# Two transformer blocks in one kernel: the second block's convolution columns go ahead of its token-shift projection

## The reference

```python
h = rms_norm(x, g[0])
p = h @ w_in_first                                   # 1024 -> 1024 + 1792 columns
y_conv = conformer_conv(p[..., :1024], ...)          # gate, 31-tap causal convolution per channel, layer norm, silu
y_rwkv, _ = rwkv7_mix(p[..., 1024:], mu, ...)        # token shift, then a recurrence over 8 heads of 64
y = concat([y_conv, y_rwkv]) @ w_out
x = x + rms_norm(y, g[1])
x = x + rms_norm(memory_cross_attention(...), g[3])
x = x + rms_norm(swiglu(...), g[5])
```

## Time and profile before

| | us |
|---|---|
| median of 3 runs | 1769.77 |
| lowest, highest | 1768.31, 1774.12 |
| the profiled execution | 1775.78 |
| span of its profile | 1773.7 |
| PE busy in the span | 1669.8 (94%) |
| DVE, ACT, POOL busy | 835.0, 605.4, 401.6 |

### The profile page before, as it was taken

One profiled execution on the slowest core, in us unless ns is written; L12 is line 12 of the kernel. 1 busy time (PEld: TensorE's weight loads), 2 busy tenths in 40 slices (PEclk: granted clock), 3 DMA queues, 4 the chain that ended last, 5 costly groups with the idle time before them and its releaser, 6 DMA issues.

```text
span 1773.7 us, 26856 instructions
## 1 busy us (share of the span) xinstructions
PE 1669.8 (94%) x11510; PEld 1373.4 (77%) x11510; DVE 835.0 (47%) x1240; ACT 605.4 (34%) x973; POOL 401.6 (23%) x349
## 2 busy tenths in 40 slices
PE   7999999999999999999898777998989899999997
PEld 6789878787888888888676666877868878888876
DVE  3377642445333333345666886635543442233234
ACT  4143432324323232343434442333434332222222
POOL 2112111112201010132135531004203431131133
PEclk7899999999999999999999889898999999999999
DMA  5123321223222222222211000014102122222221
GB/s 193 61 83 127 136 72 67 76 92 131 86 100 91 97 93 95 95 95 106 97 53 68 25 2 2 9 42 164 51 24 84 60 95 98 92 96 95 96 77 66
DMA packets 29830, 146.03 MB, mean 82 GB/s; under 512 B 4097, under 2 KB 7441, under 8 KB 14609
## 3 DMA queue, kind: packets, MB, share of 16 engines
q1 hardware_dynamic: 29712, 144.33, 23.3%
HBM read 138.03 MB, written 6.29 MB: 81 GB/s over the span
## 4 chain that ended last, share of the span: by engine, by line
PE 75%; DVE 8%; issue 7%; POOL 5%; ACT 4%; DMA 1%; POOLq 0%; SPq 0%; DVEq 0%; ACTq 0%
PE ps L153 75%; POOL zf L165 4%; DVE zf L165 2%; DVE zf L173 2%; DVE wl L165 1%; ACT zf L159 1%; ACT zr L162 1%; DVE ps L173 1%; ACT zf L162 1%; DMA raw<-in_wstream 1%; POOL tn L165 1%; ACT wh L162 1%; PE ps L156 0%; DVE zf L2326 0%; DVE zr L173 0%
## 5 line engine op out<-in xcount | busy, mean ns | idle before, releaser
L153 PE MATMUL ps<-zr,wh 128*128 128x512 f32 (+1 forms) x3936 | 1175.2, 383 | 24.7 <-DVE wl L165 13.2
L153 PEld LDWEIGHTS ps<-zr,wh 128*128 128x128 f32 x3936 | 717.8, 190 | 184.2 <-issue 11.9
L153 PE MATMUL ps<-zr,wl 128*128 128x512 f32 (+1 forms) x1968 | 745.7, 379 | 0.0
L165 POOL TENSOR_TENSOR zf<-zf 128x512 f32<-128x512 f32 (+1 forms) x253 | 295.8, 1176 | 862.0 <-ACT zf L159 581.1
L153 PEld LDWEIGHTS ps<-zr,wl 128*128 128x128 f32 x1968 | 374.1, 190 | 77.2 <-issue 0.8
L165 DVE TENSOR_TENSOR wl<-raw,wh 128x1024 fp32r<-128x1024 f32 (+1 forms) x243 | 306.4, 1300 | 231.2 <-ACT wh L162 231.0
L162 ACT ACTIVATE wh<-raw 128x1024 fp32r<-128x1024 f32 (+1 forms) x243 | 240.4, 1037 | 212.0 <-PE ps L153 210.4
L159 ACT ACTIVATE zf<-zf 128x512 f32<-128x512 f32 (+2 forms) x232 | 127.5, 560 | 399.1 <-DVE zf L165 285.1
L153 PE MATMUL ps<-zf 64*64 64x64 f32 (+6 forms) x3640 | 204.5, 249 | 34.3 <-DVE zf L165 18.7
L153 PEld LDWEIGHTS ps<-zf 64*64 64x64 f32 (+3 forms) x3640 | 163.2, 151 | 75.2 <-issue 29.1
L165 DVE TENSOR_TENSOR zf<-ps,zf 128x512 f32<-128x512 f32 (+2 forms) x133 | 84.1, 638 | 208.9 <-PE ps L153 185.6
(11 more groups left out here) (94 smaller groups left out, 725.9 us busy)
## 6 DMA issues: line engine op xcount, KB each, us to landing
raw<-in_wstream SPq DMA_DIRECT2D x117, 1024.0 KB, 4.8
zf<-in_xT SPq DMA_DIRECT2D x16, 256.0 KB, 3.1
raw<-in_wstream SPq DMA_DIRECT2D x4, 768.0 KB, 4.3
kv_scratch<-zf SPq DMA_DIRECT2D x8, 256.0 KB, 2.2
x_scratch<-zf SPq DMA_DIRECT2D x8, 256.0 KB, 2.1
zf<-x_scratch SPq DMA_DIRECT2D x8, 256.0 KB, 5.1
out<-zf SPq DMA_DIRECT2D x16, 128.0 KB, 1.7
zf<-in_cu SPq DMA_DIRECT2D x1, 1256.0 KB, 10.0
```

Of the source, the lines that this page charges most:

```text
L153: return self.raw.matmul(out_, l, x, start=start, stop=stop)
L165: return self.raw.tensor_tensor(out_, a, b, o)
```

## The change

```diff
-PFIRST = 3
...
+    for c in range(4):
+        t("cv", "w_in_first_2", 0, 8, (128 * c, 512 + 128 * c))
     for i in range(7):
         t("p", "w_in_first_2", 0, 8, [1024 + 128 * P_ORDER[2 * i + j] for j in range(2)])
-        if i == PFIRST - 1:
-            for c in range(4):
-                t("cv", "w_in_first_2", 0, 8, (128 * c, 512 + 128 * c))
...
-    for i in range(4):
-        put("ev.p", i)
-        pl.rel("D", "t.p", i)
-        if i:
-            p_tile(i - 1)
+    for i in range(2):
+        for j in range(2):
+            put("ev.cv", 2 * i + j)
+            pl.rel("D", "t.cv", 2 * i + j)
+        put("cv.mix", i)
+        mark("hc", i)
...
-            for tap in range(LAST[i] + 1):
-                while tap == LAST[i] and i > 1 and not has(("pdone",)):
-                    yield
+            for tap in range(LAST[i] if i > 1 else LAST[i] + 1):
                 put("tap.v", i, tap)
                 yield
+            if i == 1:
+                pl.rel("M", "conv.acc", i)
+        while not has(("pdone",)):
+            yield
+        for i in range(2, 4):
+            put("tap.v", i, LAST[i])
             pl.rel("M", "conv.acc", i)
+            yield
...
-    pl.pace[cv1], pl.pace[cv2] = 4, 3
+    pl.pace[cv1], pl.pace[cv2] = 6, 4
...
-    due = 3
-    for uu in range(2, 7):
-        if uu == PFIRST:
-            for i in range(4):
...
-            pl.pace[cv1] = 3
+    for i in range(2, 4):
+        n = pl.next_unit("cv")
+        pl.tile(n, 0, 2 * i)
+        if i == 3:
+            put("cv.mix", 2)
+            mark("hc", 2)
+        pl.tile(n, 1, 2 * i + 1)
+    pl.pace[cv1] = 4
+    due = None
+    for uu in range(7):
```

More of the change, by code:

```diff
@@ L515, in p_tile @@
         mark("p", P_ORDER[i])
-    n = pl.next_unit("p")
+    n = pl.next_unit("cv")
     pl.pair(n, 0)
@@ L523, in schedule @@
     put("pset")
-    n = pl.next_unit("p")
-    pl.take("D", "t.p", 2)
+    n = pl.next_unit("cv")
+    pl.take("D", "t.cv", 2)
     put("mm", n, 0, 2, 0)
@@ L528, in schedule @@
     put("mm", n, 0, 2, 1)
-    pl.take("D", "t.p", 3)
+    pl.take("D", "t.cv", 3)
     put("mm", n, 1, 3, 0)
@@ L756, in schedule @@
                 p_tile(due)
-            if i == 2 * PFIRST:
+            if i == 0:
                 put("cv.mix", 3)
```

## The result

| | before | after |
|---|---|---|
| median, us | 1771.0 (4 runs) | 1802.6 (4 runs) |
| lowest, highest | 1768.3, 1774.1 | 1801.2, 1804.6 |
| profiled execution, its span | 1775.8, 1773.7 | 1803.4, 1801.4 |

The account below looks back on a forecast made before the run. PE was taken as the bound, busy 94% of the span, with 75.5 us lost in a 389 us stretch. Waits of 26 and 51 us made 77, so +1.5 on the median of 1769.8: 1771 us, range 1751 to 1788.

Parts of the forecast that it names:

- the rule: A DVE operation with two SBUF inputs and a GpSimd operation exclude each other; one waits out the other's whole instruction.
- rival 3: POOL's additions block DVE's weight splits beside the dense tiles: 15 us, giving 1786 us; chance 0.08.
- A: First part of the second block's recurrence before the change, 819 to 991 us, holding 20 dense tiles.
- The waits of A': The first part after the change, keeping its 20 dense tiles: 146 us of work plus 26 of waits, 172 us.
- Weight splits, 5 us: Beside the dense tiles, weight remainders come 1 to 2.5 us late for three or four units: 5 us.
- The norm of pair 0, 12.5 us: At `prep`'s norm for pair 0, PE waits for ACT, ACT for DVE's scan behind its queue: 12.5 us.
- Transposes and banks, 5 us: `head 0` turns on three M banks instead of four, so products wait for evacuations: 5 us.
- Clock, 3.5 us: Work lost to PE's lowered clock beside the dense tiles, half of the earlier 6 us lost: 3.5 us.
- B' 20, C' 3, T' 28: Waits in 12 rounds without dense work, then 18 with it, then the last 19 without: 20, 3 and 28 us.
- Rival 2: The naked end, from the second quarter of `wb` on, loses 42 us instead of 28: 1785 us; chance 0.23.
- Rival 1: DVE's lag never reaches PE, so the part with the dense tiles takes 156 us: 1755 us; chance 0.33.
- The sum of +1.5 us: Over the whole stretch, waits total 77 us instead of 75.5, so the change costs 1.5 us.

Follow-up runs that it names:

- e5: Changed kernel with each of POOL's convolution additions replaced by eight zero fillings of 128x128: 1780.8 us, ratio 1.0033.
- e1: Changed kernel with POOL's convolution additions on 64 of 512 columns, the rest left out: 1777.0 us, ratio 1.0025.
- e18: Changed kernel with additions on 64 columns and two instead of four DVE taps per tile beside the projection: 1771.3 us, ratio 0.9990.
- e2: Kernel before the change with POOL's convolution additions on 64 of 512 columns, the rest left out: 1764.3 us, ratio 0.9953.
- e3: Changed kernel with each of POOL's convolution additions replaced by two zero fillings of 128x512: 1779.9 us, ratio 1.0045.

## Why the prediction was wrong

- *The step that failed* is the weighing of the rule, and with it rival 3: "Nine splits in A times 1.64 us (4.00 less 2.36) are 15 us: 1786. One in nine did so now, which speaks against." The one in nine was taken for a chance. It was the phase between ACT's queue and POOL's additions in the old order, and the change replaces this order. The trace of before had it, in rows of ACT and POOL that I did not read beside the earlier trace rows: POOL's row of 2.72 us from 901.62 ends 0.15 us after the remainder starts at 904.19. Nor could every remainder have met one: in A's trace there are ten pairs, and the first four start before POOL's first addition, at 877.04.
- *Its size.* Contention costs the changed kernel 27.3 us (ratios 1.0179 and 1.0025 of 1771), the kernel before 8.3 (0.9953), so the move pays 19 of its 32 us for it (17 by the medians). Of its sign, remainders of 4 us in most units, came four of ten above 4 us and two more at 3.4 and 3.5. Rival 3 counted remainders only, at 15; they took 34.7 us in A' where 24.4 is free (e5), 10 more. It left out the `x2` products (5.1 us, which now meet additions), the token shifts, the gates, the scan and products of `prep`, and POOL's own delay.
- *The waits of A'* were 62.2 us for 26: 13.4 at the splits, 17.3 at the norm of pair 0, 15.4 of other idling and 16.1 by the clock, for 5, 12.5, 5 and 3.5. PE's work was 142.4 for 146. The four items below take them in turn, with e1 beside them.
- *Weight splits, 5 us:* 13.4 in the waits, with 3.5 in e1, where hardly anything blocks. The sum of DVE's load was near.
- *The norm of pair 0, 12.5 us:* 17.3, and 10.2 in e1. Near for the kernel that was summed; e18 shows that 6.9 of the 10.2 hang on DVE's taps.
- *Transposes and banks, 5 us:* all other idling in A' is 15.4 us, and 11.7 in e1, so this was short in either case. Two waits behind the norm, for ACT and for DVE, are 4.4 and 4.2 of it. What of them is the third bank was not tested.
- *Clock, 3.5 us:* 16.1, and 10.0 in e1. This term was short in either case. PE's clock stood at half for 54.6 us of A', after the long waits, where it was 13.6 before.
- *B' 20, C' 3, T' 28:* 20.3, 2.0 and 21.8. Rival 2, whose point was 60 us from the second quarter of `wb` on, got 52.4 and falls. Rival 1 falls with the norm's wait.
- *The sum of +1.5 us* describes a change that meets no contention, made against a kernel that has it. e1, with A' 177.2 for 172, comes out at +4.4 us. There is luck in that: its waits in A' are 35.4 us and not 26, its work is 4 us less than forecast, and T' waits 21.7 and not 28.

What is left of the move without additions is 12.7 us (e1 against e2). The taps beside the projection are about half of that, as e18 takes 5.7 away. The other half was not taken apart.

## What to carry to other kernels

Where DVE and POOL share work, list DVE's operations with two inputs in SBUF and see, in the order of the engine that feeds POOL, what POOL does when each is issued: a reordering can turn meetings that are rare (one pair in ten here) into common ones (six in ten). Count the lock on both sides, since what is taken from DVE's wait comes back as POOL's and through whoever waits for POOL. And try the move with the suspected work made short in both kernels; here two such runs (e1, e2) put a number on a rival that had been given 0.08.

## What the hardware showed that I had not expected

- In a split two engines alternated instruction by instruction: each DVE piece waited out one addition (2.29 and 2.31 us for 1.22) and each addition one piece (1.84 and 2.09 for 1.27).
- The blocked time stands inside the instruction's own duration, and no idle time and no releaser is shown for it. It is seen only by comparing durations of one form: POOL's one `tensor_scalar` over 128x512 took 3.59 us in the changed kernel, 2.00 before and 1.57 in e1.
- A short addition pays in full: one over 64 columns, 0.32 us otherwise, took 1.29 us when the scan had been issued 0.04 us ahead of it (1.22 us).
- A filling of 128x512 on POOL took 0.53 us and one of 128x128 0.21, and neither delayed DVE's remainders (1.22 us each in e3 and e5). The records of short fillings overlap: eight of 0.21 are done in 1.23 us.
